# Softmax probabilities divided by ScalarE in the step behind the exponential, with VectorE's reciprocal ahead of the next maximum

## What is computed

```python
# first block, both attentions
logits = jnp.einsum('bqhd,bkhd->bhqk', qb, k) * scale      # + decay and mask, or + bias
p = jax.nn.softmax(logits, axis=-1)
out = jnp.einsum('bhqk,bkhd->bqhd', p, v)
# second block, window attention
p = softmax(concatenate([s_meta, s_band, s_sink], axis=-1))
of = einsum(p[..., :N_META], vm) + einsum(p[..., N_META:N_META + NB], vb)
```

## Time and profile before

| what | value |
|---|---|
| median of 3 runs | 2114.03 us (2112.88 to 2117.27) |
| profiled execution | 2113.68 us |
| its span, first to last instruction | 2111.9 us |
| mean granted TensorE clock | 0.98 |
| PE, busy | 1989.3 us, 94% of the span |
| VectorE, busy | 1008.2 us, 48% |
| ScalarE, busy | 728.0 us, 34% |

### The profile page before, as it was taken

How to read it: one execution, slowest core, us unless ns; L and a number is a source line. 1 busy time by engine, 2 the same in 40 slices (tenths; PEclk the granted TensorE clock), 3 DMA queues, 4 the chain that set the end, 5 groups by cost and what they waited for, 6 DMA issues and landing times.

```text
span 2111.9 us, 26805 instructions
## 1 busy us (share of the span) xinstructions
PE 1989.3 (94%) x10909; PEld 1671.7 (79%) x10909; DVE 1008.2 (48%) x1364; ACT 728.0 (34%) x972; POOL 23.9 (1%) x45
## 2 busy tenths in 40 slices
PE   5999999996999999989999999798999999999997
PEld 3787887873777778869999999687888777888885
DVE  7688753436555552254443322576423444444322
ACT  2455444325444432242222212455323332222111
POOL 0000000000000000000000000000000000000000
PEclk8999999998999999999999999999999999999999
DMA  6644213220232222212222223211122222222221
GB/s 266 207 162 141 90 61 121 99 80 0 83 106 89 79 88 95 96 40 94 85 82 97 74 91 104 72 61 41 41 80 80 100 80 99 94 88 90 94 89 62
DMA packets 34847, 195.45 MB, mean 93 GB/s; under 512 B 3680, under 2 KB 3696, under 8 KB 19552
## 3 DMA queue, kind: packets, MB, share of 16 engines
q1 hardware_dynamic: 29008, 173.55, 23.2%
q0 software_dynamic: 5776, 21.02, 2.9%
HBM read 192.46 MB, written 2.10 MB: 92 GB/s over the span
## 4 chain that ended last, share of the span: by engine, by line
PE 81%; DVE 11%; ACT 4%; issue 3%; DMA 1%; ACTq 0%; SPq 0%; DVEq 0%
PE PS L577 80%; DVE W_lo L1590 3%; ACT W_hi L1151 2%; DVE INV L1634 1%; DVE N L1639 1%; DMA A_low<-in_wada 1%; PE PS L723 1%; DVE T L2035 1%; DVE T L2026 1%; ACT T L1151 1%; ACT L1151 1%; DVE A_high L2069 1%; DMA ring<-in_wada 0%; DVE ring L2069 0%; ACT H_hi L1151 0%
## 5 line engine op out<-in xcount | busy, mean ns | idle before, releaser
L577 PE MATMUL PS<-H_hi,W_hi 128*128 128x512 f32 (+1 forms) x1976 | 634.1, 355 | 56.9 <-DVE H_lo L1622 19.6
L577 PE MATMUL PS<-H_hi,W_lo 128*128 128x512 f32 (+1 forms) x1976 | 633.6, 354 | 0.0
L577 PE MATMUL PS<-H_lo,W_hi 128*128 128x512 f32 (+1 forms) x1976 | 632.5, 354 | 0.0
L1590 DVE TENSOR_TENSOR W_lo<-W_raw,W_hi 128x2048 fp32r<-128x2048 f32 (+2 forms) x170 | 353.1, 2077 | 329.5 <-ACT W_hi L1151 328.8
L577 PEld LDWEIGHTS PS<-H_hi,W_hi 128*128 128x128 f32 x1976 | 350.3, 191 | 120.7 <-issue 42.8
L1151 ACT ACTIVATE W_hi<-W_raw 128x2048 fp32r<-128x2048 f32 (+2 forms) x170 | 295.5, 1738 | 321.8 <-PE PS L577 320.8
L577 PEld LDWEIGHTS PS<-H_hi,W_lo 128*128 128x128 f32 x1976 | 349.9, 191 | 49.9 <-issue 0.2
L577 PEld LDWEIGHTS PS<-H_lo,W_hi 128*128 128x128 f32 x1976 | 349.8, 191 | 49.8 <-issue 0.2
L577 PE MATMUL PS<-G_hi,W_hi 128*128 128x512 f32 (+1 forms) x704 | 209.6, 338 | 1.3 <-DVE W_lo L1590 1.3
L577 PE MATMUL PS<-G_hi,W_lo 128*128 128x512 f32 (+1 forms) x704 | 210.2, 339 | 0.0
L577 PE MATMUL PS<-G_lo,W_hi 128*128 128x512 f32 (+1 forms) x704 | 209.3, 338 | 0.0
(11 more groups left out here) (246 smaller groups left out, 2090.1 us busy)
## 6 DMA issues: line engine op xcount, KB each, us to landing
W_raw<-in_wts SPq DMA_DIRECT2D x119, 1024.0 KB, 4.7
W_raw<-in_wdown SPq DMA_DIRECT2D x48, 704.0 KB, 4.1
ring<-in_wada POOLq DMA_DIRECT2D x32, 512.0 KB, 3.8
A_high<-in_wada SPq DMA_DIRECT2D x6, 1024.0 KB, 18.0
A_low<-in_wada SPq DMA_DIRECT2D x2, 1024.0 KB, 10.6
X<-in_xT SPq DMA_DIRECT2D x2, 1024.0 KB, 10.4
X<-in_xT POOLq DMA_DIRECT2D x1, 2048.0 KB, 8.7
out<-N SPq DMA_DIRECT2D x8, 256.0 KB, 2.1
```

Source lines behind the costliest of these rows:

```text
L577: return nc.tensor.matmul(*a, **kw)
L1590: vector.tensor_tensor(W_lo[:, c.odd, 0:size], W_raw[:, c.odd, 0:size], W_hi[:, c.odd, 0:size].bitcast(FP32), ALU.subtract).then_inc(w_lo, 1)
```

## The change

In both attentions the multiplication of the probabilities goes from VectorE to ScalarE, as a copy in place with the reciprocal as its scale, behind the rounding of unit t-2 and ahead of the exponential of t. On VectorE the reciprocal of t-1 (in the window attention with the sum that it needs) now stands ahead of the maximum of t. All semaphores keep their names and their counts.

```diff
@@ ScalarE, front_steps
                                  ).then_inc(sem("f_hi"), 1)
+                    u = t - 1
+                    if 0 <= u < UNITS:
+                        w = P * (unit(u)[4] + 1)
+                        act.wait_ge(sem("f_inverse"), u + 1)
+                        activate(PR[:, u % 3, 0:w], PR[:, u % 3, 0:w], ACT.Copy, scale=fstat[:, 2, u:u + 1]
+                                 ).then_inc(sem("f_normed"), 1)
                     if t < UNITS:
@@ ScalarE, win_steps
                                  ).then_inc(sem("att_hi"), 1)
+                    u = t - 1
+                    if 0 <= u < WIN_UNITS:
+                        w = win_width(win_unit(u)[4])
+                        act.wait_ge(sem("att_inverse"), u + 1)
+                        activate(PRW[:, u % 3, 0:w], PRW[:, u % 3, 0:w], ACT.Copy, scale=stat[:, 2, u:u + 1]
+                                 ).then_inc(sem("att_normed"), 1)
                     if t < WIN_UNITS:
@@ VectorE, front_steps
                 for t in range(UNITS + 7):
+                    u = t - 1
+                    if 0 <= u < UNITS:
+                        dve.wait_ge(sem("f_prob"), u + 1)
+                        vector.reciprocal(fstat[:, 2, u:u + 1], fstat[:, 1, u:u + 1]).then_inc(sem("f_inverse"), 1)
                     if t < UNITS:
                         w = P * (unit(t)[4] + 1)
                         dve.wait_ge(sem("f_scores"), t + 1)
                         vector.tensor_reduce(fstat[:, 0, t:t + 1], score_bank(t)[:, 0:w], AX.X, ALU.max, negate=True
                                              ).then_inc(sem("f_max"), 1)
-                    u = t - 1
-                    if 0 <= u < UNITS:
-                        w = P * (unit(u)[4] + 1)
-                        dve.wait_ge(sem("f_prob"), u + 1)
-                        vector.reciprocal(fstat[:, 2, u:u + 1], fstat[:, 1, u:u + 1]).then_inc(sem("f_inverse"), 1)
-                        dve.wait_ge(sem("f_inverse"), u + 1)
-                        vector.tensor_scalar(PR[:, u % 3, 0:w], PR[:, u % 3, 0:w], fstat[:, 2, u:u + 1], None, ALU.mult
-                                             ).then_inc(sem("f_normed"), 1)
@@ VectorE, win_steps
                     if t == 2:
                         back_values()
+                    u = t - 1
+                    if 0 <= u < WIN_UNITS:
+                        dve.wait_ge(sem("att_prob"), u + 1)
+                        dve.wait_ge(sem("att_sink"), u + 1)
+                        vector.tensor_tensor(stat[:, 5, u:u + 1], stat[:, 1, u:u + 1], stat[:, 4, u:u + 1], ALU.add
+                                             ).then_inc(sem("att_total"), 1)
+                        dve.wait_ge(sem("att_total"), u + 1)
+                        vector.reciprocal(stat[:, 2, u:u + 1], stat[:, 5, u:u + 1]).then_inc(sem("att_inverse"), 1)
                     if t < WIN_UNITS:
...
-                    u = t - 1
-                    if 0 <= u < WIN_UNITS:
-                        w = win_width(win_unit(u)[4])
-                        dve.wait_ge(sem("att_prob"), u + 1)
-                        dve.wait_ge(sem("att_sink"), u + 1)
-                        vector.tensor_tensor(stat[:, 5, u:u + 1], stat[:, 1, u:u + 1], stat[:, 4, u:u + 1], ALU.add
-                                             ).then_inc(sem("att_total"), 1)
-                        dve.wait_ge(sem("att_total"), u + 1)
-                        vector.reciprocal(stat[:, 2, u:u + 1], stat[:, 5, u:u + 1]).then_inc(sem("att_inverse"), 1)
-                        dve.wait_ge(sem("att_inverse"), u + 1)
-                        vector.tensor_scalar(PRW[:, u % 3, 0:w], PRW[:, u % 3, 0:w], stat[:, 2, u:u + 1], None, ALU.mult
-                                             ).then_inc(sem("att_normed"), 1)
```

## The result

The changed kernel takes 2118.9 us (median of 18 runs, 2115.3 to 2122.8), the kernel before 2114.3 beside it (18 runs, 2111.3 to 2117.3): ratio 1.0023, 95% interval 1.0016 to 1.0030. So it is slower, by some 4.6 us and just over the 0.2% that I had named as the bound, where I forecast +1.5 us and "no difference". The time lies in my range, but 3.4 us above the likeliest value and 0.9 above the band that I had given 0.60.

What follows compares the result with a forecast made beforehand. PE, busy 94% of the span, was taken as the bound. Front +0.1 and window attention +1.4 gave +1.5 us on the profiled 2113.68, so 2115.2, or 2115.5 for the median; range 2107.5 to 2122.

Steps and rivals of the forecast that it cites:

- the band that I had given 0.60: Whole kernel: the likeliest case, a time of 2111 to 2118 us, chance 0.60.
- Prices of the copies: ScalarE: one copy in place takes 717 ns at 512 columns, 0.61, 0.50, 0.39 us when narrower, and 0.51 at 272.
- The walk through the front: Front, 95 to 326 us: shifts of PE's waits step by step, losses 4.3 and gains 4.2, sum +0.1 us.
- steps 18, 34, 56, 60: Front: W_hi a copy later in steps 16 and 32, 0.20 + 0.22; ScalarE's line in steps 55 and 59, 0.38 + 0.23.
- The start: Front: reciprocal(0) and copy(0) now lie between the first two exponentials, so the scores of step 2 come 0.65 us later.
- the idles at 136.95 and 193.10: Front: the remainder PT_lo comes 0.5 us sooner and 0.23 us of PE idle goes, gain 0.46 us.
- steps 22 to 25: Front: VectorE's gain of 0.46 us pays for the copies; scores of step 24 +0.13, the second wait gives 1.30.
- The window stretch: Window attention, 1384 to 1488 us: ScalarE's copies lose 3.55, VectorE's shorter list gains 2.15, net +1.4 us.
- The triple of steps 8, 16 and 24: Window attention: ScalarE's longer line takes 5.23 us from scores to scores instead of 4.83, loss 0.4, three times.
- the output matmuls of steps 10 and 18: Window attention: W_hi stands behind copy(7), so these matmuls come later by 0.43 and 0.41 us.
- So the idle moves from the second wait to the first: gain 1.24: Front, steps 8 and 9: scores lose 1.16 us to ScalarE's copies, then the transposes stop waiting for VectorE, gaining 1.24.
- Rival 1: ScalarE becomes the bound: copies cost more in line, VectorE's credit is spent; losses alone +7.8 us, 2121.9; chance 0.22.

## Why the prediction was wrong by 3 us, and where it was right

**Prices of the copies.** Right to 1 ns at 512 and 384 columns and at 272 (509).

**The walk through the front.** Right in most terms, where the clock holds. Shifts of PE in the second trace of the changed kernel: step 8 +1.12 and step 9 -1.12 (forecast +1.16, -1.24); step 40 +1.12 and step 41 -1.09 (+1.17, -1.07); steps 18, 34, 56, 60 +0.30, +0.29, +0.35, +0.17 (+0.20, +0.22, +0.38, +0.23). The start, from the first maximum to the second exponential, is 1.32 us for 0.68: +0.64 (0.65). Two terms were mis-sized: the idles at 136.95 and 193.10 gave 0.97, not 0.46; and at steps 22 to 25 the gain came early (-0.85 at step 23), the scores of step 24 then lost 1.14, not 0.13. Sum about -0.2, against my +0.1, and -0.22 and +0.17 measured without falls, in the two kernels with the filling matmuls.

**The window stretch.** +1.47, +1.43, +1.41 and +1.40 in four kernels with this window, against my +1.4. The triple of steps 8, 16 and 24 is +0.64 with -0.26 ahead of it, so +0.38 (0.4); the output matmuls of steps 10 and 18 +0.59 and +0.58, less 0.18 (0.43, 0.41); step 28 +0.88, step 29 -0.82 (0.71, 0.91); the gain at step 14 was 0.41 (0.63). (My list of losses adds up to 3.51, not 3.55; the net stays +1.4.) These terms are off by up to 0.2 us and the sum by less, so a part of the agreement is luck. All four have one fall in this stretch, as before has; the second trace of the changed kernel, with five, has +4.72.

**The step that failed** is "So the idle moves from the second wait to the first: gain 1.24", and its twins at steps 25 and 41: the idle moves, but the gain isn't always kept. The sum added shifts at the 2.4 GHz level throughout, as before's rows showed no other in the front. But the change doesn't only shift idle, it gathers it: two idles of 0.53 and 1.23 became one of 1.65, with the same total. Behind such an idle PE may run at 1.2 GHz for some 3.4 us, and the dense matmuls that should have used the gain take twice as long. With all 64 copies in the front I have executions with no, one, two and three falls there: -0.22 and +0.17 (with the fillings), +1.27 (front only), +2.31 and +4.13 us (the changed kernel). A fall thus costs 1.2 to 1.4 us, and the executions without any are the forecast.

**Does this carry the median?** The mean granted clock over the whole span is 0.9791 in 29 executions of the changed kernel and 0.9808 in 64 of the kernel before. 0.0017 x 2118 = 3.6 us; one fall makes up 3.4 x 0.5 = 1.7 of that, so there are about two falls more per execution, some 2.6 us. With the 1.2 to 1.5 of the walk it makes 3.8 to 4.1 of the measured 4.3 to 4.6. With the fillings the mean clock is 0.9812, that of before beside it 0.9813, and the loss 1.7. The rest, about half a microsecond, is within the intervals. One thing doesn't fit: the front alone, with the same lists and the same waits there, has 0.9805 and loses 1.3 us, the window alone 0.9806 and 1.6. The lower mean clock shows only with both halves together, and no run shows why. The clock isn't all, though: the kernels without division and with the reciprocal first have 0.9788 and 0.9795 and are faster than before in spite of it, and in the window stretch their traces have 13.7 and 10.2 us at 1.2 GHz, where before's has 3.4.

**The rivals.** Rival 1 had the side right, but for another reason: the copies are not dearer in line and VectorE's credit is not spent. The rule of the Trainium skill that spoke for it ("ScalarE: Activation LUTs", "Rules for kernel authors": multiplications on VectorE) gave the sign and not the cause. 59 of the 64 copies in the front cost nothing there: with them on ScalarE, PE's place moved by -1.99 us from step 4 to the end of the front, with none (the reciprocal moved alone) by -1.64. As a whole, though, the kernel with five units on VectorE took 2115.52 and that with all of them there 2112.07, so the rule held for the time.

**What stays open.** Which idles lead to a fall. The three traces with all 64 copies and no fillings have twelve idles of 1.64 to 2.25 us at steps 2, 8, 24 and 40, and a fall stands behind six of them: 1.65 us did twice (steps 8 and 40 of one execution) and didn't four times (of the two others, one at 1.64), 2.03 at step 24 did in two and didn't in one, and in the front-only kernel an idle of 2.25 us at step 2 did not. I can give a price and a frequency, no rule. Why the two halves together lose 1.4 to 1.7 us more than the sum of each alone, and whether the fall near 1680 us belongs to the change, is open too. That a 4-byte shift slows the matmuls on M_hi was seen in one kernel and gone in its twin; I didn't vary the shift.

## What to carry to other kernels

When a change moves idle time from one wait to the next, add up not only the sums but the longest single idle of PE: one of 1.65 us can cost more than two of 0.53 and 1.23, because the clock may fall behind it. Don't judge a difference of a few microseconds by one pair of traces; line the same instruction up in both and look at the granted clock wherever their distance jumps. And before moving work to another engine, run the kernel without it: here it was worth 2.5 us, and the new order of two small instructions alone gave 2.3.

## What the hardware showed that I had not expected

PE's clock fell to 1.2 GHz in a stretch where PE is busy for 96% of the time, behind idles of 1.65 to 2.2 us, in some executions and not in others; a fall lasted 3.4 us and cost some 1.3, and behind idles of 3.5 to 4.1 us at step 2, in three of the other kernels, it lasted 6.8. 18 more matmuls, adding zero in the idle, took 2.6 to 2.9 us off the loss (by the medians). GpSimd took 1564 ns for a multiplication of 512 columns by a value per partition, and 603 for 128: 2.5 ns a column, where VectorE needs 0.49 us for all 512. The Trainium skill ("GPSIMD Engine Reference", "4.1 Engine selection") calls one-input operations there roughly line-rate; the measurement says three times VectorE's time. A matmul of 512 columns reading a tile moved by 4 bytes took 408 for 396 ns.
